# Mixture of experts on one core: the gate and up slots of a step loaded by one 2 MB transfer instead of two of 1 MB

## The reference, cut to what matters

```python
def moe_swiglu(t, router, w_gate, w_up, w_down):
    logits = (t @ router).astype(jnp.float32)
    top_logits, top_idx = lax.top_k(logits, TOP_K)
    gates = jax.nn.softmax(top_logits, axis=-1)
    combine = jnp.sum(jax.nn.one_hot(top_idx, N_EXPERTS, dtype=jnp.float32) * gates[..., None], axis=1)
    ...
```

## Time and profile before

| | |
|---|---|
| median of 3 runs | 2262.67 us (2259.7 to 2262.86) |
| profiled execution, its own time | 2257.96 us |
| its span, first to last instruction | 2256.1 us |
| mean granted TensorE clock | 0.929 |
| busy: PE, PEld, DVE, ACT | 85%, 74%, 66%, 50% |
| expert stage | 759 to 1790 us of the span |
| HBM read | 466.33 MB |

### The profile page before, as it was taken

The page is one execution under the profiler, slowest core; times in us unless marked ns, Lnnn a source line. Parts: engine busy times, 40 slices in busy tenths (PEclk is TensorE's granted clock), DMA queues, the critical chain, the costliest instruction groups (busy, mean ns, idle before and its releaser), DMA issues.

```text
span 2256.1 us, 27763 instructions
## 1 busy us (share of the span) xinstructions
PE 1924.9 (85%) x11147; PEld 1669.3 (74%) x11148; DVE 1485.9 (66%) x1482; ACT 1134.2 (50%) x1160; POOL 33.2 (1%) x84
## 2 busy tenths in 40 slices
PE   6747867999888699999999999999999769468846
PEld 5637757999877588787878888787878659367836
DVE  3477543545454488888888888888888544744473
ACT  3241123334344476767676766767676434433441
POOL 0010000000001000000000000000000000100010
PEclk9978988999999799999999999999999979788968
DMA  7100022555320488889898888888898635113400
GB/s 288 62 0 1 1 75 99 182 186 187 112 94 14 176 352 346 344 338 357 334 363 339 351 345 346 349 341 347 335 363 353 246 130 184 38 55 116 147 0 19
DMA packets 64062, 469.18 MB, mean 208 GB/s; under 512 B 7232, under 2 KB 7360, under 8 KB 7360
## 3 DMA queue, kind: packets, MB, share of 16 engines
q1 hardware_dynamic: 63936, 467.41, 53.5%
HBM read 466.33 MB, written 1.05 MB: 207 GB/s over the span
## 4 chain that ended last, share of the span: by engine, by line
PE 80%; DVE 12%; ACT 4%; issue 2%; DMA 1%; POOL 0%; SPq 0%; ACTq 0%; DVEq 0%
PE bank L474 78%; PE bank L484 2%; ACT arena L1018 1%; DVE squares L1364 1%; ACT split_ring L1018 1%; ACT moe_pair_high L1018 1%; DVE ycat L1362 1%; DMA weight_ring<-w_dram 1%; DVE split_ring L1377 1%; DVE expert_out_low L1767 0%; DVE arena L1413 0%; ACT L1018 0%; ACT squares L1018 0%; DVE arena L1394 0%; DVE operand_low L1384 0%
## 5 line engine op out<-in xcount | busy, mean ns | idle before, releaser
L1742 DVE TENSOR_TENSOR moe_pair_low<-weight_ring,moe_pair_high 128x2048 fp32r<-128x2048 f32 x224 | 504.7, 2286 | 19.5 <-ACT moe_pair_high L1018 18.8
L474 PE MATMUL bank<-operand_high,split_ring 128*128 128x256 f32 x2464 | 467.1, 291 | 56.4 <-DVE operand_low L1384 52.0
L474 PEld LDWEIGHTS bank<-operand_high,split_ring 128*128 128x128 f32 x2464 | 401.9, 200 | 60.3 <-DVE operand_low L1384 55.1
L1377 DVE TENSOR_TENSOR split_ring<-weight_ring,split_ring 128x2048 fp32r<-128x2048 f32 x98 | 224.4, 2292 | 327.3 <-ACT split_ring L1018 327.2
L1018 ACT ACTIVATE moe_pair_high<-weight_ring 128x2048 fp32r<-128x2048 f32 x224 | 423.6, 1917 | 26.6 <-DMA weight_ring<-w_dram 25.9
L1018 ACT ACTIVATE arena<-bank 128x256 f32<-128x256 f32 (+3 forms) x275 | 129.5, 476 | 593.4 <-PE bank L474 555.8
L474 PE MATMUL bank<-moe_pair_high,operand_high 128*128 128x512 f32 x896 | 355.6, 397 | 8.3 <-DVE operand_low L1749 7.3
L474 PE MATMUL bank<-operand_low,split_ring 128*128 128x256 f32 x1232 | 357.4, 290 | 0.0
L474 PE MATMUL bank<-moe_pair_high,operand_low 128*128 128x512 f32 x896 | 353.1, 394 | 0.0
L474 PE MATMUL bank<-moe_pair_low,operand_high 128*128 128x512 f32 x896 | 351.5, 392 | 0.0
L1018 ACT ACTIVATE split_ring<-weight_ring 128x2048 fp32r<-128x2048 f32 x98 | 186.9, 1910 | 206.2 <-PE bank L474 196.2
(11 more groups left out here) (234 smaller groups left out, 2190.6 us busy)
## 6 DMA issues: line engine op xcount, KB each, us to landing
weight_ring<-w_dram SPq DMA_DIRECT2D x382, 1024.0 KB, 6.9
arena<-w_dram SPq DMA_DIRECT2D x56, 1024.0 KB, 4.8
parameters<-param_dram SPq DMA_DIRECT2D x1, 2896.5 KB, 23.4
constants<-const_dram SPq DMA_DIRECT2D x1, 2788.0 KB, 17.0
hT<-x_dram SPq DMA_DIRECT2D x1, 1024.0 KB, 4.8
out_dram<-squares SPq DMA_DIRECT2D x1, 1024.0 KB, 3.9
constants<-const_dram SPq DMA_DIRECT2D x1, 128.0 KB, 4.6
parameters<-param_dram SPq DMA_DIRECT2D x1, 54.5 KB, 4.4
```

Of the source, the lines that this page charges most:

```text
L474: return pe.matmul(out, lhsT, rhs, start=start, stop=stop, skip_group_check=True)
L1377: tt(split_ring[k][:, :], raw_slot(k), whi[n % 2][:, :].bitcast(F32), ALU.subtract).then_inc(split[late], 1)
L1742: tt(low_, raw_, high_.bitcast(F32), ALU.subtract).then_inc(moe_split, 1)
```

## The change

Gate and up of a step are loaded by one transfer, issued where gate was; the call for up does nothing. The pair has one semaphore, which both halves wait for, so the high part of gate waits for all 2 MB.

```diff
-        gate_landed, up_landed = [[sem(f"moe_{k}_landed{i}") for i in range(PAIRS)] for k in ("gate", "up")]
+        pair_landed = [sem(f"moe_pair_landed{i}") for i in range(PAIRS)]
...
             k = q % PAIRS
-            return (gate_landed if kind == "gate" else up_landed)[k], q // PAIRS + 1, len(range(k, QN, PAIRS))
+            return pair_landed[k], q // PAIRS + 1, len(range(k, QN, PAIRS))
...
             def moe_load(kind, q):
 
-                sp.dma_start(moe_place(kind, q)[0], w_dram[moe_row(kind, q)]).then_inc(moe_landing(kind, q)[0], 16)
+                n = moe_row(kind, q)
+                if kind == "gate":
+                    k = 2 * (q % PAIRS) * SLOT
+                    sp.dma_start(ring[:, k:k + 2 * SLOT].rearrange("p (g n) -> p g n", g=2), w_dram[n:n + 2].rearrange("g p n -> p g n"))\
+                      .then_inc(pair_landed[q % PAIRS], 16)
+                elif kind == "down":
+                    sp.dma_start(moe_place(kind, q)[0], w_dram[n]).then_inc(down_landed[q % 2], 16)
```

## The result

The changed kernel takes 2274.2 us (median of 6 runs, 2272.4 to 2279.55), the kernel before in the same sessions 2262.77 us (6 runs, 2257.44 to 2266.56). The ratio is 1.0058, with a 95% interval of 1.0041 to 1.0076: slower by 11.4 us. The profiled execution has a span of 2270.8 us, 14.7 over that of before.

What follows compares the result with a forecast made beforehand. The prediction took PE (TensorE's matmuls at L474) to set the pace, with DMA having some 14% to spare. Stalled steps 6.6 plus changes of expert 3.4 made 10.0 us, 2262.67 to 2272.7, say 2273 us; range 2262 to 2295.

Steps and rivals of the forecast that it cites:

- The transfer lands when up's did: Expert-stage loads: the 2 MB pair lands when up lands now, 9.5 us after its issue, up to 10.7 in late steps.
- A: Rival: the pair lands sooner than up does now, in under 9 us, so not slower, 2260 to 2266 us; chance 0.24.
- rival B: The pair lands later than up does now, over 9.9 us after issue, hence 2280 to 2320 us; chance 0.19.
- C: Rival: the pair's transfer is spread badly, over two engines, 43 us each, over 6,000 us in all; chance 0.02.
- 6.5 us from landing to PE: Serial chain behind the pair's landing: ScalarE's high part 1.95, VectorE's low parts 2.20 and 2.29, some 0.06 to PE.
- waits for the low parts in most steps: Sign of a later landing: PE waits for `moe_pair_low` in most steps, with the pair landing over 9.9 us after issue.
- 13 stalled steps, 6.6 us: Steps 4 to 111 without the seven at changes of expert: 13 late landings stall PE, largest 0.97 us, together 6.6 us.
- The changes of expert, 3.4 us: At seven changes of expert, gate half, `expert_out_low` and PE move: 4.6 us, 1.2 behind an earlier stall, leaving 3.4 us.
- No snowball: Expert stage: a stalled step does not delay the next step's data, whose loads are issued already; no term added.
- The sum: 6.6 + 3.4 = 10.0 us on the runs' median of 2262.67, so 2272.7, say 2273 us, 0.4% slower.
- No gain from the saved issue: SP issues one load fewer per step, 0.36 to 0.43 us; worth nothing, since SP waits 858.9 us for PE.

Runs made afterwards that it cites:

- the fastest version: Kernel before (two 1 MB loads) with VectorE making expert_out_low ahead of gate's low part at a change of expert: 2251.87 us, ratio 0.9964.
- the 256 KB transfer: Changed kernel with an extra 256 KB transfer to a spare place between the down slot and the pair of each burst: 2358.85 us, ratio 1.0445.

## Why the prediction was right, point by point

**The transfer lands when up's did.** Right: 9.4 us after the issue (median), where 9.5 was forecast, and 10.8 in step 5 (issue at 800.79, high parts at 811.59), where up to 10.7 was. In the trace of before, the up slot lands 9.5 us after gate's issue (median). Nothing was won by having one transfer instead of two, and with two loads and a joint wait the loss is the same within the intervals. Rivals A, B and C fell with this number.

**6.5 us from landing to PE.** Right to the hundredth in step 5. Of how much the steps have to spare, though, the prediction says too little: it gives ordinary steps 0.5 to 0.8 us, "so from about 0.7 us all of them pay". By its own sum over the trace of before, 31 of the 101 ordinary steps have between 0 and 0.8 us, 57 have more and 43 of these over 2 us. The prices of later landings were added up from the steps and do not rest on that sentence, but the sign of rival B, waits for the low parts in most steps, does: even with the landing 2.9 us later PE waited for the pair's low parts 48 times.

**13 stalled steps, 6.6 us.** The steps were named from late landings in the trace of before. PE waited for low parts 9 times, one of them the wait of step 2 that stood there before, 5.0 us in all against the 10 to 16 times and 6 to 7 us forecast. The eight new ones are steps 5, 28, 54, 57, 72, 83, 86 and 110, each of them on the list; step 8 came in time by 0.05 us, and steps 16, 27, 98 and 99, also on it, had no late landing this time. A stall costs more than its wait, though: the wait is counted from the end of a matmul, 0.40 us after its start, while the next could have started after 0.23, and the first matmul behind a stall takes 0.50 instead of 0.40. With 0.27 us for each of eight stalls the 4.0 us of new waiting become 6.2. So the term came out near its 6.6 by two errors: five steps fewer stalled, and each stall cost more than the prediction gave it. The late landings stay at the same steps, which speaks for something that follows the program, as its instruction fetches do. The trace of before bears that out: in 47 of steps 4 to 111 a packet of the instruction queue starts while gate or up is on its way, and among them are 21 of the 23 steps in which up landed over 9.9 us after its issue; in the fastest version it is 48, with all 21 of the late ones. More than half of those 47 steps have no late landing, and no run moved the fetches, so the link is likely and not shown by an experiment.

**The changes of expert, 3.4 us.** Nearly right in size, with a term missing. PE's waits for `expert_out_low` rose by 1.9 us, not by 3 to 4, and the longest of them, 2.4 us, brought a further loss that I had not priced. The rows are PE's of the changed kernel, at that wait and behind it:

```profile
1053.43 0.50 PE L474 MATMUL bank<-moe_down_high,hidden_high 128*128 128x512 f32 x1 [2.36 <-DVE expert_out_low L1767]
1053.77 0.39 PE L474 MATMUL bank<-moe_down_low,hidden_high 128*128 128x512 f32 x1
1054.00 0.45 PE L474 MATMUL bank<-moe_down_high,hidden_low 128*128 128x512 f32 x1
1054.24 0.63 PE L474 MATMUL bank<-moe_down_high,hidden_high 128*128 128x512 f32 x1
1054.67 0.63 PE L474 MATMUL bank<-moe_down_low,hidden_high 128*128 128x512 f32 x1
```

Starts 0.23 us apart become 0.43 us apart, until 1057.64, eight matmuls and 1.5 us in all. The window from 1054.00 to 1057.60 has a granted clock of 0.53, so nearly all of it the lower level, 1.2 GHz. A wait of nearly the same length, at the last change of expert, was followed by no such fall (the wait, then the window behind it, with the granted clock as third number from its end):

```profile
1696.33 0.50 PE L474 MATMUL bank<-moe_down_high,hidden_high 128*128 128x512 f32 x1 [2.23 <-DVE expert_out_low L1767]
```

```profile
1696.30:1700.00 3.70, 3.67 (x16) 3.00 (x17) 3.70 (x4) 2.35 (x3) 0.00 (x0) 1.00 0.31 128
```

The gather, for which the prediction has no term, paid 0.6 us once, ahead of step 37. With 1.9 for the waits, 1.5 for the clock and 0.6, this group costs 4.0 us where 3.4 stood.

**No snowball.** Right: the loads of the next step are issued already, and the step behind a stalled one has over a microsecond to spare. The step of the sum that would have failed for a larger delay is the other one: with the 256 KB transfer steps stall one after another, and the whole costs 98 us, far less than the stalls of all steps taken one by one would (some 190 in the ordinary steps alone, by the same sum with the landing 3.4 us later).

**The sum.** 6.2 and 4.0 make 10.2. 10.0 us were forecast, 10.2 is what the stage of the profiled execution took more from its first gate/up matmul to its last one's (1000.78 to 1010.96 us), and 11.4 the runs. Terms that were too high and terms that were missing met in the middle; the agreement to 1 us is partly luck.

**No gain from the saved issue.** Right: SP still waits for PE, 894.3 us of the stretch from 780 to 1780 us ahead of its down loads.

## What to carry to other kernels

Merging two transfers moves the landing of the first half to that of the second. Where the transfers of a burst already follow each other without a gap, nothing is gained, and what counts is the first consumer's wait: add the serial chain behind the new landing and hold it against each step's own deadline, late landings included. Issue slots in the order in which they are used, and look for the wait that ends just ahead of PE, here `expert_out_low`: a swap of two instructions on VectorE won 8.5 us, when none of the rearrangements of loads tried here won anything.

## What the runs showed of the hardware

A stall of PE can cost more than itself, since the granted clock may fall with it: 2.4 us of waiting were followed by 3.6 us at a granted clock of 0.53, and 1.5 us more were lost. The length of the wait alone does not decide it. From step 3 to the last step of the stage the clock fell 21 times in the ten profiles, each time at a PE wait of at least 1.88 us; six other waits of 1.8 to 2.9 us, the 2.23 us of the changed kernel among them, brought no fall, and after the stalls of under 1 us in ordinary steps the clock stayed at its higher level.

A small transfer in a full queue costs more than its bytes. An extra 64 KB in rows of 512 bytes moved the pair's landing by 1.0 us, and 256 KB in rows of 2 KB by 2.9 us; at the rate of the slots (1 MB in 2.5 us) they would have been 0.2 and 0.6 us. The packets themselves explain a part of it. A 512-byte packet took 27 ns (median), 19 bytes per ns, a 2 KB packet 106 ns, again 19, and an 8 KB packet of the slots 309 ns, 26.5 bytes per ns; over 16 engines the mean packet times make 0.3 and 1.3 us per extra transfer. What the rest is, no run shows. That the second also held the down slot issued ahead of it (4.8 to 6.8 us) fits a queue that has not drained when the next burst comes. The Trainium skill ("DMA: Bandwidth & Descriptors", Specifications) asks for at least 512 bytes per piece for the full rate; the 512-byte rows here met that and did not reach the 26.5 bytes per ns of the 8 KB rows.
